# Padding the rows of one matmul operand and moving three others by a few bytes

## The chip, the cores and the metric

The kernel runs on one core of a Trainium2 chip. The metric is the device time of one execution, in microseconds (us). Three runs of the kernel before took 2669.15, 2674.47 and 2677.79 us; their median is 2674.47.

## The reference, cut to what matters

One layer of a decoder for 256 prompt tokens and 32 sample tokens (8 sequences of 4), 288 columns in all, at width 2048. Three sub-layers follow one another, each modulated (shift, scale, gate) by a conditioning vector:

```
sh1, sc1, gt1, sh2, sc2, gt2, sh3, sc3, gt3 = adaln_params(c, w_ada, b_ada)
x = x + MACARON * gt1 * swiglu(modulate(x, g_ffn1, sh1, sc1), w1_ffn1, w3_ffn1, w2_ffn1)
heads, state = mixer(modulate(x, g_mix, sh2, sc2))
x = x + gt2 * (heads @ w_out)
x = x + MACARON * gt3 * swiglu(modulate(x, g_ffn2, sh3, sc3), w1_ffn2, w3_ffn2, w2_ffn2)
```

`modulate` is an RMS norm with a gain and a shift, `swiglu(h, w1, w3, w2)` is `(silu(h @ w1) * (h @ w3)) @ w2` with an inner width of 5504 (43 tiles of 128). The mixer projects to q, k and v, attends with eight forgetting heads and eight dilated-window heads over the prompt or over a cache of 1024 tokens, and joins the heads. All is float32.

## The kernel before, in words

**Layout.** Features lie on the 128 partitions, tokens along the free dimension, so an activation is a tile of 16 k-tiles (2048 / 128) by T = 288 columns. `x` is the residual. A normalized activation is kept as two parts whose sum is its value: `h_hi` (rounded to the matmul's format, float32r) and `h_lo` (what is left), each [128, 16, 288] (L172). The inner activation of a feed-forward has the same form in `g_hi` and `g_lo`, up to 15 k-tiles of 288 columns (L190). A weight tile lands in `raw` (two slots of 16 x 128 columns), ScalarE writes its rounded part to `w_hi` (`split_high`, L867), VectorE the rest to `w_lo` (`split_low`, L1095).

**The product.** For each output tile of 128 features and for each k-tile, TensorE makes three products into one bank (`products`, L556 to L565): `w_hi` with `h_hi` (L562), `w_hi` with `h_lo` (L563), `w_lo` with `h_hi` (L564). Each loads a weight slice of 128 columns (512 bytes a partition) and then streams 288 columns (1152 bytes a partition). In the second half of a feed-forward `g_hi` and `g_lo` stand in place of `h_hi` and `h_lo`.

**Stages.** The conditioning parameters first (about 110 us), then the first feed-forward with the rest of the conditioning between its products, in three chunks of 15, 14 and 14 inner tiles, each an `up` and a `down` part (to 1089 us), the projections (1103 to 1433), the attention (to 1724), the output projection (to 1830), and the second feed-forward (1844 to 2670). `up`, projections and output projection read h, `down` reads g.

**What orders it.** Each engine runs its own program, and semaphores that the kernel names itself (L275 to L283) are the only waits between engines; nothing is derived from tiles. SP issues the weight loads in the order of their use, two slots ahead.

**Memory.** `at` (L157) puts a tile at a given byte of each partition, and `sb` (L160) takes the next free byte and rounds the tile's size up to 32 bytes. So every tile's address follows from the order and sizes of the calls: `x`, `h_hi`, `h_lo`, `par`, the constants, `raw`, `w_hi`, `w_lo`, then at `mix0` (L188) `g_hi`, `g_lo` and the rest. Before, in bytes of a partition: `h_hi` 34944, `h_lo` 53376, `w_hi` 97472, `w_lo` 113856, `g_hi` 130240, `g_lo` 147520, and the end at 229376. The attention lays its own tiles over parts that are idle then: `kv_raw` and `kv_high` over the rings from `raw` on, `kv_h` over the upper halves of `h_hi` and `h_lo`, `kv_z` over `mix0`.

**Small scalars.** `nw4`, `eps`, `bfs`, `mx`, `nm`, `sm`, `rs`, `pmx` and `psm` are one to four columns each (L180 to L266): norm weights, a constant, and the maxima and sums of the attention's softmax. Each takes 32 bytes of its own.

**Writers of h_hi.** In the norms ScalarE copies four k-tiles at once (L900) and VectorE subtracts (L1127); in the attention single k-tiles and blocks of 16 columns are written (L1016, L1069, L1324, L1411).

Of the kernel before, what the change touches and what calls it, by code (L numbers as in the profile page):

```python
# [31 lines left out]
F32R = mybir.dt.float32r  # L32
# [5 lines left out]
P = 128  # L38
D = 2048
KT = D // P  # L40
HEADS, HD = 8, 128
TP, NB, NS = 256, 8, 4
TS = NB * NS
T = TP + TS
FF = 43
CHUNKS = ((0, 15), (15, 14), (29, 14))
NPAR = 9
# [98 lines left out]
def decoder_layer(nc, xT, cT, gT, bada, nwT, bfg, relb, pt, cst, cst2, ohrev, addrev, selh,  # L146
# [7 lines left out]
    with ExitStack() as ctx:  # L154
        top = [16512]

        def at(name, shape, dt, off):  # L157
            return nc.alloc_sbuf_tensor_at(name, shape, dt, offset=off)

        def sb(name, shape, dt=F32):  # L160
            n = int(np.prod(shape[1:])) * 4
            t = at(name, shape, dt, top[0])
            top[0] += -(-n // 32) * 32
            return t
# [4 lines left out]

        x = sb("x", [P, KT, T])  # L170
        h0 = top[0]
        h_hi, h_lo = sb("h_hi", [P, KT, T], F32R), sb("h_lo", [P, KT, T], F32R)  # L172
        par = sb("par", [P, ADA * NC])
        c0 = top[0]
        sc32 = sb("sc32", [P, KT, 32])
        lf = at("lf", [HEADS, T], F32, c0)
        cs = sb("cs", [P, C_SMALL])
        gv = sb("gv", [P, 3, KT])
        ba = sb("ba", [P, ADA])
        nw4 = sb("nw4", [P, 4])  # L180
        nw = sb("nw", [P, 32])
        eps = sb("eps", [P, 1])
        ident, ones, sel9 = cs[:, C_ID:C_ID + P], cs[:, C_ONE:C_ONE + P], cs[:, C_SEL:C_SEL + NC]

        rings0 = top[0]
        raw = sb("raw", [P, 2, KT * P])
        w_hi, w_lo = sb("w_hi", [P, 2, KT * P], F32R), sb("w_lo", [P, 2, KT * P], F32R)
        mix0 = top[0]  # L188

        g_hi, g_lo = sb("g_hi", [P, 15, T], F32R), sb("g_lo", [P, 15, T], F32R)  # L190
        adaw = sb("adaw", [P, 2, KT * P])
        part_sb = sb("part_sb", [P, 4 * P])
        su, gf = sb("su", [P, T]), sb("gf", [P, T])
        hf = sb("hf", [P, 2, SQL, T])
        sq = sb("sq", [P, 2, SQL, T])
# [40 lines left out]
        def quad(name, *offs):  # L236

            n = GB // len(offs)
            parts = [at(f"{name}_{i}", [P, n, HEADS * P], F32, o) for i, o in enumerate(offs)]
            return [parts[j // n][:, j % n, :] for j in range(GB)]  # L240
        half = HEADS * T * 4
# [3 lines left out]
        first_v = at("kv_first_v", [P, 2, HEADS * P], F32, vn0)  # L245
        first = [first_v[:, 0, :], first_v[:, 1, :], at("kv_first_a", [P, HEADS * P], F32, hf0)[:, :],
                 at("kv_first_b", [P, HEADS * P], F32, sel0 + 5120)[:, :]]
        third = [quad("kv_h", h0 + half, h0 + 3 * half), quad("kv_z", mix0)]
        assert GB // 2 * HEADS * P * 4 <= half

        def kv(m, j):
# [8 lines left out]
        qbd = [sb("qbd0", [P, 2, 288]), at("qbd1", [P, 2, 288], F32, over + 13440)]  # L260
        assert 32768 + 13440 + 2304 <= 6 * KT * P * 4
        lft = at("lft", [P, 3, HEADS], F32, c0 + T * 4)
        bfs = sb("bfs", [HEADS, 1])
        rbs = sb("rbs", [32, HEADS])
        mx, nm, sm, rs = sb("mx", [P, 2]), sb("nm", [P, 2]), sb("sm", [P, 2]), sb("rs", [P, 2])
        pmx, psm = sb("pmx", [P, 2, 2]), sb("psm", [P, 2, 2])  # L266
        rev_dram = nc.dram_tensor("rev_dram", [HEADS, P, REV], F32).ap()

        pairs = [ctx.enter_context(nc.psum_tensor(f"banks{i}", [P, 2, 512], F32)) for i in range(4)]
# [1162 lines left out]
def _tiles(w, k, n):  # L1432

    return np.ascontiguousarray(w.reshape(k, P, n, P).transpose(2, 1, 0, 3).reshape(n, P, k * P))
# [62 lines left out]
def _lay_out(i):  # L1497
# [6 lines left out]
    def up(w1, w3):  # L1504
        return np.ascontiguousarray(np.stack([_tiles(w1[0], KT, FF), _tiles(w3[0], KT, FF)], 1).reshape(2 * FF, P, KT * P))

# [18 lines left out]
                                   .reshape(ADA, P, KT * P)),  # L1525
        w13_1=up(a["w1_ffn1"], a["w3_ffn1"]), w2_1=_tiles(a["w2_ffn1"][0], FF, KT),
        w_in=_tiles(cat(cols, 1), KT, 49), w_out=_tiles(a["w_out"][0], KT, KT),
        w13_2=up(a["w1_ffn2"], a["w3_ffn2"]), w2_2=_tiles(a["w2_ffn2"][0], FF, KT),

# [38 lines left out]
```

## Time and profile before

| what | value |
|---|---|
| median of three runs | 2674.47 us |
| profiled execution, first to last instruction | 2673.7 us, 0.8 us under that median |
| TensorE matmuls busy | 2522.4 us (94%) |
| weight loads busy | 2321.7 us (87%) |
| VectorE, ScalarE busy | 1159.7 us (43%), 919.7 us (34%) |
| mean granted TensorE clock | 0.962 |
| DMA moved | 614.13 MB, 230 GB/s in the mean |

The profile is of one execution and holds no other time of it than that span. Matmuls overlap in it: each lasts some 295 ns by the records, but the next one starts after some 132 ns, so what a product costs is read from the distance between starts, not from durations. Weight loads overlap the matmuls of the product before.

### The profile page before, as it was taken

What the parts mean: (1) busy time and instruction counts of PE and PEld (TensorE: products, weight loads), DVE (VectorE), ACT (ScalarE), POOL (GpSimd) and SP (SyncE); (2) the same over time, 40 slices, a digit from 0 to 9 for tenths busy, and PEclk for the clock granted to TensorE, in tenths of its full rate; (3) what the DMA queues carried; (4) which work ended last, traced back from release to release, by engine and by line L of the source; (5) the groups of instructions that cost most, each with busy time, mean ns of one, the idle gap of its engine ahead of it and who ended that gap; (6) DMA issues with size and microseconds to landing.
All of it is one profiled execution on the core that took longest, in us unless ns stands there. A gap on an engine that the chain in (4) does not pass through costs nothing.

```text
span 2673.7 us, 53818 instructions
## 1 busy us (share of the span) xinstructions
PE 2522.4 (94%) x20995; PEld 2321.7 (87%) x20995; DVE 1159.7 (43%) x1767; ACT 919.7 (34%) x1155; POOL 44.6 (2%) x86
## 2 busy tenths in 40 slices
PE   6898999999999999899999777797999999999999
PEld 3597999999999999799997343597999999999999
DVE  0343444444444445666652111255444544454444
ACT  1432323233333334566541112245333333333332
POOL 0130000000000000000000000000000000000000
PEclk7798999999999999999999878898999999999999
DMA  8887777777767764344456999943444444454444
GB/s 355 341 313 230 286 267 286 275 283 267 289 219 281 277 230 162 128 157 150 164 210 256 389 361 408 349 161 125 161 168 165 165 165 165 159 171 165 165 159 159
DMA packets 105867, 614.13 MB, mean 230 GB/s; under 512 B 16192, under 2 KB 16464, under 8 KB 56128
## 3 DMA queue, kind: packets, MB, share of 16 engines
q1 hardware_dynamic: 101728, 603.81, 61.5%
q0 software_dynamic: 4064, 9.26, 1.3%
q8 instruction: 54, 0.88, 0.1%
q14 instruction: 21, 0.17, 0.0%
HBM read 604.36 MB, written 8.66 MB: 229 GB/s over the span
## 4 chain that ended last, share of the span: by engine, by line
PE 87%; DMA 8%; SPq 2%; DVE 1%; ACT 1%; issue 1%; ACTq 0%; DVEq 0%
PE banks L562 26%; PE banks L563 25%; PE banks L564 25%; PE banks L503 4%; DMA adax<-in_w_ada_dram 2%; PE banks L830 1%; PE banks L787 1%; DMA adaw<-in_w_ada_dram 1%; SPq L440 1%; DMA kv_raw<-in_vpool_dram 1%; PE banks L514 1%; DMA raw<-in_w_dram 1%; PE banks L649 1%; PE banks L661 0%; PE banks L773 0%
## 5 line engine op out<-in xcount | busy, mean ns | idle before, releaser
L562 PE MATMUL banks<-h_hi,w_hi 128*128 128x288 f32 x3792 | 1129.1, 298 | 28.6 <-DVE h_lo L1127 23.1
L563 PE MATMUL banks<-h_lo,w_hi 128*128 128x288 f32 x3792 | 1122.6, 296 | 0.0
L564 PE MATMUL banks<-h_hi,w_lo 128*128 128x288 f32 x3792 | 1121.2, 296 | 0.0
L1095 DVE TENSOR_TENSOR w_lo<-raw,w_hi 128x1024 fp32r<-128x1024 f32 (+2 forms) x666 | 763.8, 1188 | 378.7 <-ACT w_hi L867 372.4
L867 ACT ACTIVATE w_hi<-raw 128x1024 fp32r<-128x1024 f32 (+2 forms) x666 | 667.8, 1030 | 554.0 <-PE banks L564 507.3
L562 PEld LDWEIGHTS banks<-h_hi,w_hi 128*128 128x128 f32 x3792 | 717.0, 189 | 50.2 <-issue 43.7
L563 PEld LDWEIGHTS banks<-h_lo,w_hi 128*128 128x128 f32 x3792 | 716.9, 189 | 0.8
L564 PEld LDWEIGHTS banks<-h_hi,w_lo 128*128 128x128 f32 x3792 | 716.3, 189 | 0.0
L562 PE MATMUL banks<-g_hi,w_hi 128*128 128x288 f32 x1376 | 409.2, 297 | 0.0
L563 PE MATMUL banks<-g_lo,w_hi 128*128 128x288 f32 x1376 | 406.8, 296 | 0.0
L564 PE MATMUL banks<-g_hi,w_lo 128*128 128x288 f32 x1376 | 406.6, 296 | 0.0
L562 PEld LDWEIGHTS banks<-g_hi,w_hi 128*128 128x128 f32 x1376 | 259.5, 189 | 5.4 <-issue 5.4
L563 PEld LDWEIGHTS banks<-g_lo,w_hi 128*128 128x128 f32 x1376 | 259.5, 189 | 0.0
L564 PEld LDWEIGHTS banks<-g_hi,w_lo 128*128 128x128 f32 x1376 | 259.5, 189 | 0.0
L908 ACT ACTIVATE part_sb<-banks 128x256 f32<-128x256 f32 (+1 forms) x64 | 26.3, 410 | 438.1 <-PE banks L503 438.1
L936 ACT ACTIVATE su<-banks 128x288 f32<-128x288 f32 x86 | 35.4, 412 | 403.6 <-PE banks L564 403.6
L1204 DVE TENSOR_TENSOR gf<-su,banks 128x288 f32<-128x288 f32 x86 | 39.1, 454 | 225.5 <-PE banks L564 225.5
L1149 DVE TENSOR_TENSOR par<-banks,ba 128x18 f32 (+3 forms) x64 | 11.5, 179 | 276.2 <-PE banks L514 276.2
L503 PE MATMUL banks<-adaw,sc 128*32 128x256 f32 x1792 | 112.2, 391 | 12.8 <-DMA adaw<-in_w_ada_dram 12.8
L1193 DVE TENSOR_TENSOR tmps<-banks,par 128x32 f32<-128x32 f32 x112 | 21.4, 191 | 232.8 <-PE banks L564 232.8
L503 PEld LDWEIGHTS banks<-adaw,sc 128*32 128x32 f32 x1792 | 53.1, 111 | 53.9 <-DMA adaw<-in_w_ada_dram 13.4
L503 PE MATMUL banks<-adax,sc 128*32 128x256 f32 x512 | 49.3, 534 | 29.5 <-DMA adax<-in_w_ada_dram 29.4
(186 smaller groups left out, 1134.7 us busy)
## 6 DMA issues: line engine op xcount, KB each, us to landing
raw<-in_w_dram SPq DMA_DIRECT2D x172, 1024.0 KB, 4.8
adaw<-in_w_ada_dram SPq DMA_DIRECT2D x112, 1024.0 KB, 6.4
raw<-in_w_dram SPq DMA_DIRECT2D x64, 896.0 KB, 4.6
raw<-in_w_in_dram SPq DMA_DIRECT2D x49, 1024.0 KB, 4.8
adax<-in_w_ada_dram SPq DMA_DIRECT2D x32, 1024.0 KB, 8.3
raw<-in_w_dram SPq DMA_DIRECT2D x32, 960.0 KB, 4.7
raw<-in_w_out_dram SPq DMA_DIRECT2D x16, 1024.0 KB, 4.8
kv_raw<-in_kpool_dram SPq DMA_DIRECT2D x24, 512.0 KB, 6.0
```

What stands on the lines that cost most here:

```text
L440: sp.dma_start(kv(m, j), src.rearrange("a p n -> p (a n)"))\
L503: last = pe.matmul(ada_part[32 * j:32 * j + 32, a:a + 2 * P], sc32[:, kt, :], w[:, k * 2 * P:(k + 1) * 2 * P], start=kt < 4, stop=kt >= KT ...
L514: last = pe.matmul(ada_selp[:, c * NC:(c + 1) * NC], part_sb[:, c * P:(c + 1) * P], sel9, start=True, stop=True)
L562: pe.matmul(bank[:, 0:T], hi, m_hi[:, k, :], start=k == 0, stop=False)
L563: pe.matmul(bank[:, 0:T], hi, m_lo[:, k, :], start=False, stop=False)
L564: last = pe.matmul(bank[:, 0:T], lo, m_hi[:, k, :], start=False, stop=k == nk - 1)
L649: last = pe.matmul(ss2[:, j, 0:T], ones, sq[:, j, SQL - 1, :], start=True, stop=True)
L787: r = pe.matmul(dst(j), qbd[j // 2][:, j % 2, 32 * h:32 * h + 32], moving(j, h), start=False, stop=h == HEADS - 1, tile_position=(0, 32 * ...
L867: act.activation(w_hi[:, r, a:b], raw[:, r, a:b], ACT.Copy).then_inc(S["hi_ready"], 1)
L936: act.activation(su[:, :], acc_a[:, 0:T], ACT.Silu).then_inc(S["acc_a_read"], 1)
L1095: dve.tensor_tensor(w_lo[:, r, a:b], raw[:, r, a:b], w_hi[:, r, a:b].bitcast(F32), ALU.subtract).then_inc(S["lo_ready"], 1)
L1204: dve.tensor_tensor(gf[:, :], su[:, :], acc_b[:, 0:T], ALU.mult).then_inc(S["acc_b_read"], 1)
```

## The change

Nothing that is computed changes, and no instruction is added or taken away. `h_hi` gets rows of 290 elements instead of 288 (1160 bytes from one k-tile to the next instead of 1152), and the kernel goes on using the first 288; `h_lo` keeps 288. `mix0`, where g begins, moves up by 32 bytes. The nine small tiles become slices of one tile `few` of 24 columns, which stands before the rings. The overlay `kv_h` follows the new halves.

```diff
+TPAD = T + 2
-        h_hi, h_lo = sb("h_hi", [P, KT, T], F32R), sb("h_lo", [P, KT, T], F32R)
+        h_hi = sb("h_hi", [P, KT, TPAD], F32R)[:, :, 0:T]
+        hl0 = top[0]
+        h_lo = sb("h_lo", [P, KT, T], F32R)
...
-        nw4 = sb("nw4", [P, 4])
         nw = sb("nw", [P, 32])
-        eps = sb("eps", [P, 1])
+        few = sb("few", [P, 24])
+        nw4, eps, bfs = few[:, 0:4], few[:, 4:5], few[0:HEADS, 5:6]
+        mx, nm, sm, rs = (few[:, 6 + 2 * i:8 + 2 * i] for i in range(4))
+        pmx, psm = (few[:, 14 + 4 * i:18 + 4 * i].rearrange("p (a b) -> p a b", a=2) for i in range(2))
...
-        mix0 = top[0]
+        mix0 = top[0] + 32
+        top[0] = mix0
...
-        third = [quad("kv_h", h0 + half, h0 + 3 * half), quad("kv_z", mix0)]
+        third = [quad("kv_h", h0 + HEADS * TPAD * 4, hl0 + half), quad("kv_z", mix0)]
...
-        bfs = sb("bfs", [HEADS, 1])
         rbs = sb("rbs", [32, HEADS])
-        mx, nm, sm, rs = sb("mx", [P, 2]), sb("nm", [P, 2]), sb("sm", [P, 2]), sb("rs", [P, 2])
-        pmx, psm = sb("pmx", [P, 2, 2]), sb("psm", [P, 2, 2])
```

The addresses that follow, in bytes of a partition:

| tile | before | after |
|---|---|---|
| `h_hi`, k-tile k | 34944 + 1152 k | 34944 + 1160 k |
| `h_lo`, k-tile k | 53376 + 1152 k | 53504 + 1152 k |
| `raw` | 81088 | 81248 |
| `w_hi` | 97472 | 97632 |
| `w_lo` | 113856 | 114016 |
| `g_hi`, k-tile k | 130240 + 1152 k | 130432 + 1152 k |
| `g_lo`, k-tile k | 147520 + 1152 k | 147712 + 1152 k |

## Rows read from the trace of the kernel before

**Rows 1.** The page: span, busy tenths and clock in 40 slices, the chain that ended last.
```profile
span 2673.7 us, 53818 instructions
...
PE   6898999999999999899999777797999999999999
...
PEclk7798999999999999999999878898999999999999
...
PE banks L562 26%; PE banks L563 25%; PE banks L564 25%; PE banks L503 4%; DMA adax<-in_w_ada_dram 2%; PE banks L830 1%; PE banks L787 1%; DMA adaw<-in_w_ada_dram 1%; SPq L440 1%; DMA kv_raw<-in_vpool_dram 1%; PE banks L514 1%; DMA raw<-in_w_dram 1%; PE banks L649 1%; PE banks L661 0%; PE banks L773 0%
```

**Rows 2.** Windows by stage: stretch, its length, busy time (count) by engine, clock, DMA share, GB/s.
```profile
core 0: us, PE busy (x) PEld busy (x) DVE busy (x) ACT busy (x) POOL busy (x), PEclk, DMA share, GB/s
250.00:500.00 250.00, 250.00 (x2156) 232.06 (x2149) 104.24 (x158) 75.86 (x94) 0.00 (x0) 0.99 0.75 277
...
1443.00:1724.00 281.00, 214.36 (x2764) 124.36 (x2763) 48.95 (x177) 54.09 (x155) 0.95 (x1) 0.84 0.97 378
2136.00:2312.00 176.00, 176.00 (x1333) 176.00 (x1332) 81.00 (x97) 62.86 (x70) 0.00 (x0) 1.00 0.47 163
2314.00:2402.00 88.00, 88.00 (x662) 88.00 (x661) 46.43 (x79) 30.08 (x32) 0.00 (x0) 1.00 0.49 163
```

**Rows 3.** Groups by line, TensorE: shapes, count, busy us, mean ns. L563 and L564 repeat these.
```profile
L562 PE MATMUL banks<-h_hi,w_hi 128*128 128x288 f32 x3792 | 1129.1, 298 | 28.6 <-DVE h_lo L1127 23.1 <-DVE w_lo L1095 5.3
...
L562 PE MATMUL banks<-g_hi,w_hi 128*128 128x288 f32 x1376 | 409.2, 297 | 0.0
```

**Rows 4.** Line L562 on h, then on g: count, duration ns min/median/max, first and last start.
```profile
L562 PE MATMUL banks<-h_hi,w_hi x445: 290/293/297, 2135.8 to 2311.9; 128*128 128x288 f32 x149
...
L562 PE MATMUL banks<-g_hi,w_hi x221: 292/295/302, 2313.9 to 2401.9; 128*128 128x288 f32 x111
```

**Rows 5.** Timeline of TensorE on g: start us, duration us, line. It repeats every fourth row.
```profile
2640.14 0.29 PE L563 MATMUL banks<-g_lo,w_hi 128*128 128x288 f32 x1
2640.27 0.29 PE L564 MATMUL banks<-g_hi,w_lo 128*128 128x288 f32 x1
2640.40 0.29 PE L562 MATMUL banks<-g_hi,w_hi 128*128 128x288 f32 x1
2640.53 0.30 PE L563 MATMUL banks<-g_lo,w_hi 128*128 128x288 f32 x1
2640.68 0.29 PE L564 MATMUL banks<-g_hi,w_lo 128*128 128x288 f32 x1
...
2641.21 0.29 PE L562 MATMUL banks<-g_hi,w_hi 128*128 128x288 f32 x1
```

**Rows 6.** Timeline of TensorE on h at half clock.
```profile
1103.52 0.44 PE L564 MATMUL banks<-h_hi,w_lo 128*128 128x288 f32 x1
1103.76 0.44 PE L562 MATMUL banks<-h_hi,w_hi 128*128 128x288 f32 x1
```

**Rows 7.** Groups by line: the writes of h_hi and their like; then the wait behind them.
```profile
L1127 DVE TENSOR_TENSOR h_lo<-hf,h_hi 128x1152 fp32r<-128x1152 f32 x12 | 16.3, 1355 | 8.4 <-ACT h_hi L900 8.3
...
L1117 DVE TENSOR_TENSOR hf<-x,y 128x1152 f32<-128x1152 f32 x12 | 16.2, 1354 | 0.2
...
L900 ACT ACTIVATE h_hi<-hf 128x1152 fp32r<-128x1152 f32 x12 | 14.0, 1166 | 0.4
...
L1069 ACT ACTIVATE h_hi<-banks 128x64 fp32r<-128x64 f32 x8 | 1.3, 220 | 18.9 <-PE banks L661 18.9
...
PE banks L562 <- DVE h_lo L1127: 23.1, 4, 10.7
```

**Rows 8.** DMA issues of equal size: count, KB each, median us to landing.
```profile
kv_raw<-in_kpool_dram SPq DMA_DIRECT2D x24, 512.0 KB, 6.0
...
kv_z<-in_wink_dram SPq DMA_DIRECT2D x16, 512.0 KB, 8.9
```

**Rows 9.** Groups by line: one of the small scalars.
```profile
L1398 DVE TENSOR_REDUCE sm<-sm 128x1 f32<-128x2 f32 x4 | 0.6, 155 | 4.3 <-ACT ps L1052 4.3
```

## The prediction

> **What bounds the kernel now.** I read the page first: the span, the slices, and the chain that ended last. TensorE is busy in nearly every slice at nearly full clock, and three lines, L562 to L564, hold 76% of the chain; no DMA and no other engine comes near them [rows 1]. The reader is to see that this is a kernel whose time is the number of its products times the pace at which they start, outside one stretch.
>
> Next I read the windows by stage. In 250 to 500 us and again in 2136 to 2402 us TensorE is never idle; from 1443 to 1724 us (the decode attention) it is the DMA that is full, 0.97, and TensorE has idle time [rows 2]. So what the change does to a product counts in full outside that stretch, and what it does to a transfer counts inside it.
>
> The counts come from the groups of instructions: each of the three lines made 3792 products on h and 1376 on g, 11376 and 4128 together, all of them 128 rows by 288 columns in the same number format [rows 3]. The paces come from one line's view in two stretches with nothing but products. On h the line runs 445 times, first to last 2135.8 to 2311.9 us: 176.1 / 444 = 0.3966 us for three products, 132.2 ns each. On g it runs 221 times in 2313.9 to 2401.9: 88.0 / 220 = 0.4000, 133.3 ns each [rows 4]. Same shape, same weights ring, same engine, and yet 1.1 ns apart: what differs is where the operands lie.
>
> The timeline of g shows how. Its starts are 0.13, 0.13, 0.13 us apart and then 0.14, and that repeats with every fourth product: 2640.14 to 2640.68 and 2640.68 to 2641.21 are four steps of 0.535 us together [rows 5]. The duration view agrees: on g some matmuls last 302 ns, on h none is over 297 [rows 4]. If the long step is 140 ns (0.14 in the rows), the three short ones are (4 x 133.3 - 140) / 3 = 131.1 ns. At half clock, at 1103 us, the same products start 0.24 us apart, which is 288 columns at 1.2 GHz and nothing on top; at full clock that would be 120 ns [rows 6]. So at full clock each product pays 11 to 20 ns that the columns do not explain, and that depends at least in part on addresses.
>
> **The change part by part.** It removes and adds no instruction. It moves addresses, and I work out four effects.
>
> *Products on h.* From the allocation: all weight slices lie a multiple of 512 bytes apart. Rows of h and g begin 1152 bytes (9 x 128) apart. Counted modulo 128 bytes from the weights, g now begins at 0 and h at 64. Afterwards g and h_lo begin at 32, and row k of h_hi at 32 + 8k, since its rows are 1160 bytes apart. The trace shows two relations, 0 (133.3 ns) and 64 (132.2 ns), and neither of the new ones, so the price is bounded from both sides. Below: 120 ns, the columns alone [rows 6], -12.2 x 11376 = -139 us. Above: every step the long one, 140 ns [rows 5], +7.8 x 11376 = +89 us. I take 131.3 ns, next to g's short step, because three of four steps of g and most of h sit there and a relation that shares nothing with the two bad ones should lose the long steps and no more: -0.9 x 11376 = -10.2 us.
>
> *Products on g.* By the same argument 133.3 goes to 131.3 ns: -2.0 x 4128 = -8.3 us. Bounds: 120 ns gives -13.3 x 4128 = -55 us, 140 ns gives +6.7 x 4128 = +28 us.
>
> What is late next if products get 1% faster: the weight split on VectorE and ScalarE, busy 81 and 63 of 176 us on h, and the weight DMA, 0.47 there and 0.75 at 250 us [rows 2]. All have room for 1%, so the gain stays.
>
> A rule speaks against both terms. The rows say that two streams with equal shapes run 1.1 ns apart. The Trainium skill, "TensorE: Matmul & The Clock Gate", section "Step-by-step: what each phase is for", says that TensorE has two independent read ports, so that loading the next weights takes no read bandwidth from the running matmul. By that rule an offset between weights and rows would cost nothing and both terms would be zero. The trace disagrees by those 1.1 ns, unless something else about the addresses makes them.
>
> *Writing and reading h_hi.* The 12 ACT copies that write it in the norms write four rows of 288 with a gap of 8 bytes where they wrote 1152 in one run. VectorE shows both kinds: L1117, whose second operand is four repeats of 288, takes 1354 ns, and L1127, all of one run, 1355 [rows 7]. So I put the rows at nothing, below and above. For ScalarE no such pair stands in the trace; its bounds are 0 and one more fixed cost for each of four rows, for which the shortest ACT row, 220 ns, is a ceiling: 12 x 0.66 = 8 us, of which only what TensorE waits for in the norms, 23.1 us in 4 waits, is exposed; I take 0 [rows 7]. The attention's writes of single rows (L1016) keep their shape.
>
> *Transfers and the small tile.* The rings move by 160 bytes, so the destinations of raw, kv_raw and kv_high no longer begin at a multiple of 64 bytes. Packets and bytes stay. Landing times of equal transfers lie between 6.0 and 8.9 us over different destinations with no order that follows the address [rows 8]. Bounds: 1% of the 281 us either way, +-2.8 us; taken 0. This has no cover in that stretch, since the DMA is the bound there. The one-column and two-column scalars keep their instructions and semaphores; L1398 takes 155 ns on two columns wherever they stand [rows 9]. The waits are written by hand on semaphores, so sharing a tile adds none. Nothing.
>
> Sum: -10.2 - 8.3 = -18.5 us on the profiled execution's span of 2673.7, which lies 0.8 us under the median of the three runs, 2674.47. On the median that is 2656 us.
>
> **The rivals.**
>
> 1. *Nothing that can be measured.* The mean pace is kept by a cycle of stalls, and new offsets only order it differently: 132.2 and 133.3 stay within 0.5 ns, at most 0.5 x 15504 = 8 us. For it: g with its long steps and h without them differ by only 0.8%, so the pace hardly depends on offsets. Against it: the long step is plainly there to be removed. Time 2666 to 2682, say 2674.
>
> 2. *A large gain.* The 11 to 20 ns above the columns are all a clash of two reads, and at 32 bytes it is gone. For it: half clock shows no such excess [rows 6]. Against it: no step in the rows here is near 120. A third of the bound is -65 us, 2610; all of it, -194, 2480.
>
> 3. *Slower: the rows of h_hi no longer share a phase.* Now every row begins at the same place modulo 128, and the pattern of steps can settle. With 1160 bytes each k begins elsewhere, half of the rows at 8 modulo 16. If that gives h the cycle of g, one long step in four, h goes to 133.3: +1.1 x 11376 = +12.5 us, 2687. If every odd row of h_hi (half of 7584 products) takes the long step, it is 7.8 x 3792 = +30 us, 2704. It decides from a mean pace on h of 132.9 ns on. For it: g shows that a long step needs only another offset [rows 5]. Against it: 64 and 0 have no feature that 32 + 8k is bound to worsen.
>
> A page points the same way. The Trainium skill, "Advanced Engine Details and Errata", section "SBUF Cachelines", gives lines of 16 bytes and a penalty for changing to another line. A row of 1152 bytes then covers 72 lines from an even start and 73 from one 8 bytes in; as an estimate from that page, 1/72 of a step on 3792 products, +7 us. No run here shows such a start yet.
>
> **How the numbers follow.** Forecast, 8 to 40 us gained: 0.40. Large gain, over 40 us: 0.14. Nothing: 0.26. Slower: 0.20. A change of 0.3% (8 us) is about what a measurement of this kernel can tell from none. So faster 0.54, same 0.26, slower 0.20. The likeliest case alone reaches from 2634 to 2666. For eight in ten I leave out half of the large gains and the upper half of the slower ones: 2605 to 2690.
>
> **What would show it.** In the trace after: line L562 on g over the stretch of its products should give 0.394 us for three, with no matmul over 297 ns, and on h 0.394 as well. If g's every fourth step is still 0.14, that term is wrong; if h is above 0.3987, rival 3 holds; if either is under 0.389, rival 2. L900 above 1.2 us or a kv landing median moved by over 5% would show the terms that I put at nothing. The prediction is wrong if the paces move and the time does not, which would mean that a wait took the gain.

## The result: slower by half a percent, and the profile after

The changed kernel takes 2689.29 us in the median of four runs (2687.06 to 2689.87), the kernel before 2675.56 us (2669.15 to 2677.79). The ratio is 1.0055, 95% interval 1.0041 to 1.0070: some 14 us slower, where 18.5 us faster was forecast. The time lies at the upper end of the range and beside the 2687 us of the third rival.

The page of the changed kernel (lines are three further down, so that L562 to L564 are L565 to L567 now):

```profile
span 2687.2 us, 53818 instructions
...
PE 2528.8 (94%) x20995; PEld 2332.2 (87%) x20995; DVE 1159.7 (43%) x1767; ACT 919.4 (34%) x1155; POOL 44.5 (2%) x86
...
L565 PE MATMUL banks<-h_hi,w_hi 128*128 128x288 f32 x3792 | 1142.5, 301 | 29.3 <-DVE h_lo L1130 22.8
```

Little else on the page has moved: counts are equal, and VectorE and ScalarE are as busy as before. The place to look is the pace. The view of line L565 over the stretch of h, then of g, that answers to [rows 4] (count, duration ns min/median/max, first and last start):

```profile
L565 PE MATMUL banks<-h_hi,w_hi x445: 291/297/302, 2146.0 to 2324.0; 128*128 128x288 f32 x149
...
L565 PE MATMUL banks<-g_hi,w_hi x222: 292/295/298, 2325.6 to 2414.0; 128*128 128x288 f32 x111
```

On h 178.0 us over 444 steps of three products is 133.6 ns a product, where it was 132.2; the longest matmul lasts 302 ns, where it was 297. On g 88.4 over 221 is 133.3 ns, as before, although its longest matmul went from 302 to 298 ns. Were this so in every stretch, the 11376 products on h would pay 1.4 ns more, 15.9 us, and the 4128 on g nothing. The span grew by 13.5 us. The start times of the two traces close the gap: in the first feed-forward, where the conditioning's products stand between, h went only from 132.3 to 133.3 ns. Summed stretch by stretch at full clock, the products on h took 13.8 us more and those on g 0.6.

The timeline of g (start us, duration us) answers to [rows 5]:

```profile
2339.72 0.30 PE L566 MATMUL banks<-g_lo,w_hi 128*128 128x288 f32 x1
2339.86 0.29 PE L567 MATMUL banks<-g_hi,w_lo 128*128 128x288 f32 x1
2339.99 0.30 PE L565 MATMUL banks<-g_hi,w_hi 128*128 128x288 f32 x1
2340.12 0.29 PE L566 MATMUL banks<-g_lo,w_hi 128*128 128x288 f32 x1
2340.26 0.30 PE L567 MATMUL banks<-g_hi,w_lo 128*128 128x288 f32 x1
```

Before, one matmul in four lasted 0.30; now every second one does, and four steps still take 0.54 us. By the start times, a cycle on g was three steps of 130 to 132 ns and one of 140; now steps of 131 to 132 and of 135 take turns. The long step is gone, and the time that it cost has been spread over the others.

On h, in the stretch of [rows 4], the start times before show no long step at all: all but three of 1341 steps are 131 to 134 ns. After, they lie between 126 and 141 ns.

The terms that were put at nothing, in the windows by stage (columns as in [rows 2]), the groups and the DMA issues ([rows 7, 8]):

```profile
1447.00:1731.00 284.00, 208.80 (x2768) 121.80 (x2766) 48.94 (x177) 53.72 (x155) 0.95 (x1) 0.87 0.97 379
2146.00:2324.00 178.00, 178.00 (x1335) 178.00 (x1333) 80.89 (x96) 62.74 (x70) 0.00 (x0) 1.00 0.46 162
```

```profile
L903 ACT ACTIVATE h_hi<-hf 128x1152 fp32r<-128x1152 f32 x12 | 14.0, 1168 | 0.4
```

```profile
kv_raw<-in_kpool_dram SPq DMA_DIRECT2D x24, 512.0 KB, 6.4
...
kv_z<-in_wink_dram SPq DMA_DIRECT2D x16, 512.0 KB, 9.6
```

The granted clock of the products on h is 1.00, as before, so the pace is not the clock's doing. ScalarE writes four padded rows in 1168 ns where it took 1166. In the attention the DMA moves 379 GB/s where it moved 378, with the queue full either way. These two landings are up by 0.4 and 0.7 us, 7 and 8%, and the one that rose most, kv_raw from in_wink_dram, went from 8.3 to 10.3; that is over the 5% that the prediction named as the sign of a cost. The cost did not come: from the last product of the projections to the first of the output projection it is 292.6 us, where it was 293.9.

### The profile page after: what moved, and what is told of

The parts are those of the page before. It is cut to its first block, busy times and chain, and to the rows that moved or that the text cites. A ratio compares the mean times of both kernels' runs of the same rounds, so it can differ in the third digit from the quotient of the medians.

```text
span 2687.2 us, 53818 instructions
## 1 busy us (share of the span) xinstructions
PE 2528.8 (94%) x20995; PEld 2332.2 (87%) x20995; DVE 1159.7 (43%) x1767; ACT 919.4 (34%) x1155; POOL 44.5 (2%) x86
## 4 chain that ended last, share of the span: by engine, by line
PE 87%; DMA 8%; SPq 2%; DVE 1%; ACT 1%; issue 1%; ACTq 0%; DVEq 0%
PE banks L565 26%; PE banks L567 25%; PE banks L566 25%; PE banks L506 4%; DMA adax<-in_w_ada_dram 3%; DMA kv_h<-in_vpool_dram 1%; PE banks L833 1%; SPq L443 1%; PE banks L790 1%; DMA adaw<-in_w_ada_dram 1%; DMA kv_raw<-in_wink_dram 1%; DMA kv_z<-in_wink_dram 1%; PE banks L517 1%; PE banks L652 1%; SPq L434 1%
## 5 line engine op out<-in xcount | busy, mean ns | idle before, releaser
L565 PE MATMUL banks<-h_hi,w_hi 128*128 128x288 f32 x3792 | 1142.5, 301 | 29.3 <-DVE h_lo L1130 22.8
L566 PE MATMUL banks<-h_lo,w_hi 128*128 128x288 f32 x3792 | 1124.1, 296 | 0.0
L567 PE MATMUL banks<-h_hi,w_lo 128*128 128x288 f32 x3792 | 1122.6, 296 | 0.0
L565 PEld LDWEIGHTS banks<-h_hi,w_hi 128*128 128x128 f32 x3792 | 716.3, 189 | 50.9 <-issue 44.9
L566 PEld LDWEIGHTS banks<-h_lo,w_hi 128*128 128x128 f32 x3792 | 721.1, 190 | 0.8
L567 PEld LDWEIGHTS banks<-h_hi,w_lo 128*128 128x128 f32 x3792 | 719.5, 190 | 0.0
L565 PE MATMUL banks<-g_hi,w_hi 128*128 128x288 f32 x1376 | 410.0, 298 | 0.0
L566 PE MATMUL banks<-g_lo,w_hi 128*128 128x288 f32 x1376 | 407.6, 296 | 0.0
L567 PE MATMUL banks<-g_hi,w_lo 128*128 128x288 f32 x1376 | 407.5, 296 | 0.0
L565 PEld LDWEIGHTS banks<-g_hi,w_hi 128*128 128x128 f32 x1376 | 259.3, 188 | 5.4 <-issue 5.4
L566 PEld LDWEIGHTS banks<-g_lo,w_hi 128*128 128x128 f32 x1376 | 259.4, 188 | 0.0
L567 PEld LDWEIGHTS banks<-g_hi,w_lo 128*128 128x128 f32 x1376 | 259.3, 188 | 0.0
```

The lines of the kernel that those rows point to most:

```text
L565: pe.matmul(bank[:, 0:T], hi, m_hi[:, k, :], start=k == 0, stop=False)
L566: pe.matmul(bank[:, 0:T], hi, m_lo[:, k, :], start=False, stop=False)
L567: last = pe.matmul(bank[:, 0:T], lo, m_hi[:, k, :], start=False, stop=k == nk - 1)
```

## The experiments

The terms used below: the distance of a row is the byte at which it begins, minus that of the weight slice, modulo 128. Before it was 64 for h and 0 for g; the change makes it 32 for g and h_lo and 32 + 8k for row k of h_hi. Paces of whole kernels come from line views like the one above, over the second feed-forward. The letters A to D and F are theories that the expectations state. Edits are against the changed kernel in the first three runs and in the padding alone, and against the kernel before in the others.

### Four parts alone

**The shift of h_lo without the pitch.**

```diff
-        h_hi = sb("h_hi", [P, KT, TPAD], F32R)[:, :, 0:T]
+        h_hi = sb("h_hi", [P, KT, T], F32R)
+        top[0] += 128
```

> The changed kernel with one part undone: rows of h_hi are 1152 bytes apart again, but h_lo keeps its new place 128 bytes later, and rings and g stay where the change put them. In the trace of the changed kernel three products on h take 0.4008 us (133.6 ns each) where they took 0.3966 (132.2), and g is as before (133.3). Theory A, halves: a product is slow where h_hi and h_lo of the same k-tile begin in different halves of 256 bytes, as g_hi and g_lo always did. Then the 128 bytes alone do it: h at 133.3 ns, some 12 us over the kernel before. Theory B, pitch: rows of 1160 bytes do it; then h is back at 132.2 and the time within 3 us of before. Theory C, weights: the distance of rows from weights modulo 64 does it; then h stays at 133.6, some 14 us over.

```profile
L566 PE MATMUL banks<-h_hi,w_hi x446: 293/296/298, 2150.9 to 2328.8; 128*128 128x288 f32 x149
```

177.9 / 445 / 3 = 133.3 ns. Time 1.0057 of before (1.0039 to 1.0074): as slow as the changed kernel. The pitch is not needed for the loss, so B as it was put falls. A and C both still stand.

**The pitch with both operands in the same half.**

```diff
-        h_hi = sb("h_hi", [P, KT, TPAD], F32R)[:, :, 0:T]
-        hl0 = top[0]
-        h_lo = sb("h_lo", [P, KT, T], F32R)
+        hl0 = top[0]
+        h_lo = sb("h_lo", [P, KT, T], F32R)
+        h0 = top[0]
+        h_hi = sb("h_hi", [P, KT, TPAD], F32R)[:, :, 0:T]
```

> The changed kernel with h_lo and h_hi allocated in the other order: h_lo at 34944 and h_hi at 53376 with rows of 1160 bytes, so that both begin in the same half of 256 bytes for every k; rings and g stay where the change put them. A, halves: h at 132.2 ns, time within 4 us of the kernel before. B, pitch: h at 133.6, some 14 us over. C, weights: 133.6, some 14 us over.

```profile
L566 PE MATMUL banks<-h_hi,w_hi x445: 292/296/300, 2152.8 to 2329.9; 128*128 128x288 f32 x149
```

177.1 / 444 / 3 = 133.0 ns, time 1.0055 (1.0038 to 1.0072). A alone asked for 132.2 and does not fit; 133.0 is none of the three numbers. The pace accounts for only 0.8 x 11376 = 9 of the 15 us: in this run's trace the stretch from the last product of the projections to the first of the output projection takes 301 us, against 294 before. Over all traces of the layer it takes 292 to 301 and does not follow where the rings lie: the changed kernel, with the same rings, has 293.

**The rings and g alone.**

```diff
-        h_hi = sb("h_hi", [P, KT, TPAD], F32R)[:, :, 0:T]
+        h_hi = sb("h_hi", [P, KT, T], F32R)
         hl0 = top[0]
         h_lo = sb("h_lo", [P, KT, T], F32R)
+        top[0] += 128
...
```

The overlay `kv_h` follows here.

> Only the rings and g are moved as in the change; h_hi and h_lo have the addresses and the rows of the kernel before. A and B: h at 132.2 ns and g at 133.3, time within 3 us of before. C, weights: h at 133.6, some 14 us over.

Line L566 over the second and the third chunk's products on h:

```profile
L566 PE MATMUL banks<-h_hi,w_hi x447: 294/294/297, 2150.0 to 2329.9; 128*128 128x288 f32 x149
...
L566 PE MATMUL banks<-h_hi,w_hi x447: 294/296/297, 2420.3 to 2598.7; 128*128 128x288 f32 x149
```

179.9 / 446 / 3 = 134.5 ns and 178.4 / 446 / 3 = 133.3 ns; time 1.0068 (1.0051 to 1.0084). With h_hi and h_lo exactly where they were before, moving the weights by 160 bytes is enough: C holds, A and B fall. And the two stretches run the same instructions on the same addresses at different paces, so addresses allow more than one pace. What picks one is not shown.

**g_lo moved by 128 bytes in the kernel before.**

```diff
-        g_hi, g_lo = sb("g_hi", [P, 15, T], F32R), sb("g_lo", [P, 15, T], F32R)
+        g_hi = sb("g_hi", [P, 15, T], F32R)
+        top[0] += 128
+        g_lo = sb("g_lo", [P, 15, T], F32R)
...
```

To make room, seven of the small scalars share one tile here, behind everything that a product reads; the runs `f1_weights48` and `f3_g64` below do the same.

> The kernel before with g_lo 128 bytes later (nothing else that a product reads is moved; the small scalars after the end of the activations share one tile to make room), so that g_hi and g_lo of a k-tile begin in the same half of 256 bytes. A, halves: g goes from 133.3 to 132.2 ns, 4128 times 1.1 ns, some 4.5 us under the kernel before. B, pitch, and C, weights: g stays at 133.3, no change.

```profile
L565 PE MATMUL banks<-g_hi,w_hi x223: 288/296/298, 2317.0 to 2405.8; 128*128 128x288 f32 x112
```

88.8 / 222 / 3 = 133.3 ns, time 1.0012 (0.9998 to 1.0026): no change. A falls once more. The distance of g is 0 modulo 128 here as before, as C needs. The shared tile of scalars costs nothing that can be measured either.

### Two maps of the pace

To see the rule itself, TensorE was run alone on other addresses. Each loop is this, with three turns; W, H and L stand for its addresses, "..." for the flags of the accumulation, and loops on the addresses of g have 14 k-tiles:

```
for j in range(2):
    for k in range(16):
        w, hi, lo, b = W + 8192 * j + 512 * k, H + 1152 * k, L + 1152 * k, banks[j][:, 0:288]
        pe.matmul(b, at(w, P), at(hi, 288), ...)
        pe.matmul(b, at(w, P), at(lo, 288), ...)
        pe.matmul(b, at(w + 16384, P), at(hi, 288), ...)
```

> Nothing of the layer is computed here: TensorE alone runs the three products of the kernel (same shapes, two weight slots, two banks) in 57 loops of 2 tiles x 16 k-tiles x 3 passes, each loop with other addresses of the weights, of the first and of the second operand; the other engines are idle. Its total time means nothing, the mean distance between starts within each loop does. If operand addresses alone set the pace, the loops with the addresses of the kernels repeat their paces: h before 132.2 ns, g before 133.3, h after 133.6, rings moved alone 133.3 to 134.4; if other engines' accesses matter, they don't. Theory C, distance of rows from weights: moving the weights by d bytes and moving both rows by -d give the same pace, and 64 modulo 128 is the fast one. Theory D, where the weight slice itself begins modulo 64: moving the weights by 32 makes it slow, moving the rows does nothing. Theory F, a cycle that locks on its history: equal addresses at the first and the last loop may differ, and the pace follows no address. Columns: if the 12 ns over the columns' own time are a fixed cost of a product, 256 columns take 118.9 ns and 512 take 225.5; if the weight load bounds the pace, 256 columns still take 130 or more and 512 take 215.

> As the first map, nothing of the layer is computed: 62 loops of products with other operand addresses, TensorE alone. Rule under test, from the first map: with rows that begin at a multiple of 32 bytes and lie 1152 apart, the pace follows the distance of the rows from the weight slices modulo 128 bytes: 64 gives 132.2 ns, 0 and 32 and 96 modulo 64 give 132.2 or 133.3, 16 and 80 give 131.1. By the rule: rows of g moved by 64 give 132.2 with the weights where they are, 133.3 with the weights at +32, and 131.1 with the weights at +48 or +112; rows +32 with weights +80, and rows +64 with weights +112, are distance 16 and give 131.1; rows +16 with weights +64 are distance 16 too, but begin at a 16: 131.1 if distance is all, above 132 if the beginning of the row counts as well. Rows of 1160 bytes for h_hi with the weights back at distance 64: 132.2 if the pitch costs nothing by itself, 132.9 (as in the first map) if it costs 0.7. A rival, that the paces are an accident of one loop, falls if the first loop, its repeat at the end and the repeats of +48 and +112 come out as before.

Lines of the first map, one a loop, where 95 steps of three products lie between first and last start. In this order: addresses of the kernel before with the weights at +32, +48, +64, +80; the rings moved alone; both rows moved by 192; 256 columns; 512 columns; and the addresses before, repeated last.

```profile
L209 PE MATMUL banks<-rows x96: 293/295/298, 413.4 to 451.4; 128*128 128x288 f32 x96
...
L218 PE MATMUL banks<-rows x96: 292/293/297, 451.8 to 489.2; 128*128 128x288 f32 x96
...
L227 PE MATMUL banks<-rows x96: 293/295/297, 489.6 to 527.6; 128*128 128x288 f32 x96
...
L236 PE MATMUL banks<-rows x96: 295/297/302, 528.0 to 566.3; 128*128 128x288 f32 x96
...
L164 PE MATMUL banks<-rows x96: 294/296/298, 222.2 to 260.2; 128*128 128x288 f32 x96
...
L353 PE MATMUL banks<-rows x96: 288/296/297, 1024.9 to 1062.9; 128*128 128x288 f32 x96
...
L551 PE MATMUL banks<-rows x96: 278/279/284, 1838.3 to 1871.6; 128*128 128x256 f32 x96
...
L614 PE MATMUL banks<-rows x96: 387/390/393, 2116.0 to 2181.5; 128*128 128x512 f32 x96
...
L623 PE MATMUL banks<-rows x96: 292/294/295, 2182.2 to 2219.9; 128*128 128x288 f32 x96
```

Such a line gives the pace to some 0.3 ns (38.0 / 285 = 133.3, 37.4 / 285 = 131.2, 38.3 / 285 = 134.4, 37.7 / 285 = 132.3). The start times of the same traces give it finer; over the last two thirds of each loop the mean distance between starts is, in ns:

| distance of the rows | 64 | 48 | 40 | 32 | 16 | 0 | 112 | 96 | 80 |
|---|---|---|---|---|---|---|---|---|---|
| weights moved by | 0 | 16 | 24 | 32 | 48 | 64 | 80 | 96 | 112 |
| ns a product | 132.22 | 132.78 | 132.22 | 133.33 | 131.11 | 133.33 | 134.44 | 132.22 | 131.11 |

| loop with the addresses of | map | in the kernel |
|---|---|---|
| h before, first map's last loop | 132.22 | 132.2 |
| g before | 133.33 | 133.3 |
| h after | 133.61 | 133.6 |
| g after | 133.33 | 133.3 |
| rings moved alone | 133.33 | 133.3 and 134.5 |
| h with the shift of h_lo, no pitch | 133.33 | 133.3 |

A lone TensorE repeats these paces, all but the 134.5 of one stretch, so they need no other engine's access and no transfer. With rows laid out as those of h, moving the weights one way or both rows the other way is the same: weights +64 and rows +192 give 133.33 both, weights +96 and rows +160 give 132.22 both, and +128 of either is back at 132.22. So in these loops it is the distance that counts, modulo 128; D, the weights' own address, falls. F falls in its plain form, since the repeated loops agree (132.22 in both maps, +48 and +112 at 131.11 in both).

The column loops fit neither of the two ideas put ahead: 116.7 ns for 256 columns and 230.0 for 512, where a fixed cost wanted 118.9 and 225.5 and a bound by the weight load 130 or more and 215. The excess over the columns' own time at full clock, 106.7 and 213.3, is 10.0 and 16.7. Addresses count here as well: with the weights at +48 the second map has 118.9 and 230.7.

Lines of the second map: rows of 1160 for h_hi with the distance of before; rows +32 with weights +80 (distance 16); rows +16 with weights +64 (distance 16 too); rows of g +64 with weights +48, then with weights +112; `h_lo` alone +128 with weights +48. The last line is of the first map: rows 1280 bytes apart.

```profile
L506 PE MATMUL banks<-rows x96: 289/296/302, 1621.0 to 1658.9; 128*128 128x288 f32 x96
...
L461 PE MATMUL banks<-rows x96: 292/293/298, 1430.4 to 1467.8; 128*128 128x288 f32 x96
...
L470 PE MATMUL banks<-rows x96: 289/295/296, 1468.2 to 1505.8; 128*128 128x288 f32 x96
...
L389 PE MATMUL banks<-rows x84: 292/293/294, 1162.8 to 1195.1; 128*128 128x288 f32 x84
...
L434 PE MATMUL banks<-rows x84: 293/296/300, 1329.6 to 1362.9; 128*128 128x288 f32 x84
...
L560 PE MATMUL banks<-rows x96: 293/294/298, 1850.5 to 1888.2; 128*128 128x288 f32 x96
...
L515 PE MATMUL banks<-rows x96: 290/293/298, 1684.8 to 1722.8; 128*128 128x288 f32 x96
```

From the start times: 133.06, 131.11, 131.67, 130.00, 133.33, 132.50 and 133.33 ns. So the pitch of 1160 costs 0.84 at the distance of before. Rows that begin at a 16 have other paces than their distance gives: 131.67 for 131.11 at 16, and in the first map 132.22 for 134.44 at 112.

The rule of distance does not carry over to g, though its rows begin at multiples of 32 too. At 0, 32 and 64 they agree with those of h, but at 16 they have 130.00 for 131.11, at 80 (weights +112) 133.33 for 131.11, and at 96 133.3 for 132.22; the expectation of 131.1 at 16 and 80 was missed both times. Nor is it the distance alone on h: with the weights at +48, `h_lo` 128 bytes later gives 132.50 for 131.11, and rows 1280 bytes apart, ten times 128, leave every distance at 64 and give 133.33 for 132.22. So where the two rows lie to one another and from one k-tile to the next counts as well, and the runs give no rule for that.

Pitches of 1168, 1184 and 1216 for both rows gave 132.08, 132.22 and 132.22 at the distance of before. With the weights at +48, where 1152 has 131.11, they gave 132.4, 132.2 and 131.11. So 1168 and 1184 are free at one distance and cost over 1 ns at another.

### The rule in whole kernels

**The padding alone, all distances as before.** Here `few` stands at the end, the rings 64 bytes later than they would then begin, and `mix0` without its 32 bytes.

```diff
-        few = sb("few", [P, 24])
+        few = at("few", [P, 22], F32, 229280)
...
+        top[0] += 64
         rings0 = top[0]
...
-        mix0 = top[0] + 32
+        mix0 = top[0]
```

> The padding of h_hi alone: rows of 1160 bytes, h_lo 128 bytes later, and the weights and g moved so that every distance modulo 128 bytes is that of the kernel before (64 for h_lo and the first row of h_hi, 0 for g); the small scalars stand behind the other tiles. If the 32 bytes of distance explained all, h is at 132.2 and the time within 3 us of before. If the pitch costs something by itself, as the second map has it (133.06 at these addresses): 11376 x 0.84 = some 9.5 us over, g unchanged at 133.3.

```profile
L567 PE MATMUL banks<-h_hi,w_hi x446: 289/296/302, 2146.0 to 2323.7; 128*128 128x288 f32 x149
```

177.7 / 445 / 3 = 133.1 ns, time 1.0046 (1.0032 to 1.0059). By these paces the pitch costs 0.9 x 11376 = 10 us of these 12.

**g at the distance of h.**

```diff
-        mix0 = top[0]
+        mix0 = top[0] + 64
+        top[0] = mix0
```

> The kernel before with g alone 64 bytes later, so that its rows stand at distance 64 from the weights, as those of h do. By the maps g goes from 133.3 to 132.2 ns, 4128 x 1.1 = 4.6 us under the kernel before, h unchanged; by the theory that g is slow for its two halves (which the run with g_lo moved already speaks against) nothing changes.

```profile
L564 PE MATMUL banks<-g_hi,w_hi x221: 290/293/295, 2308.6 to 2395.9; 128*128 128x288 f32 x111
```

87.3 / 220 / 3 = 132.3 ns, time 0.9971 (0.9958 to 0.9984): 8 us faster, 4 to 11, where 4.6 was expected.

**Weights 48 bytes later, g 64 bytes later.**

```diff
-        w_hi, w_lo = sb("w_hi", [P, 2, KT * P], F32R), sb("w_lo", [P, 2, KT * P], F32R)
+        wts = sb("wts", [P, 4 * KT * P + 16], F32R)
+        w_hi, w_lo = (wts[:, 12 + n * 2 * KT * P:12 + (n + 1) * 2 * KT * P].rearrange("p (r n) -> p r n", r=2) for n in range(2))
...
-        over = rings0 + 32768
+        over = rings0 + 32768 + 64
```

> The kernel before with the weight slices 48 bytes later and g 64 bytes later, rows of h as they were (1152 apart). The second map has 131.1 ns for h and 130.0 for g at these addresses. If what the maps show of a lone TensorE holds beside working engines and transfers: h 131.1, g 130.0, so 11376 x -1.1 and 4128 x -3.3 = -12.5 - 13.8 = some 26 us under the kernel before. Rival, that the kernel's other stages or the weight split take it back: under 8 us. Rival, that the maps do not carry over: paces stay between 132 and 134, no change.

```profile
L564 PE MATMUL banks<-h_hi,wts x445: 292/293/298, 2124.1 to 2298.8; 128*128 128x288 f32 x149
...
L564 PE MATMUL banks<-g_hi,wts x222: 292/294/298, 2299.9 to 2387.8; 128*128 128x288 f32 x111
```

h at 174.7 / 444 / 3 = 131.2 ns, as mapped; g at 87.9 / 221 / 3 = 132.6, not the 130.0 of the map. The time is 2662.41 us against 2676.1, ratio 0.9959 (0.9944 to 0.9974): some 11 us, 7 to 15, under the kernel before. Some 26 us had been expected. By the paces, 11376 x 1.0 + 4128 x 0.7 = 14 us; most of what is missing is g, (132.6 - 130.0) x 4128 = 11 us. It is the fastest of the versions by its median; whether it beats the one with g alone moved, 2667.85, these intervals do not tell.

## Why the prediction was wrong

*The bound was read rightly.* The pace of the products accounts for the time: 13.8 us on h and 0.6 on g, against a span that grew by 13.5.

*The step that failed is the value taken for both terms.* The prediction took 131.3 ns because "a relation that shares nothing with the two bad ones should lose the long steps and no more". That treats the long step as a stall on top of a fixed short step. On g the long step did go, and the mean stayed at 133.3 ns to the tenth: every second step grew to 135. The short step of a slow cycle is not the pace of another cycle. For h the ground was misread as well: "most of h" does not sit at 131.3. Of those 1341 steps on h before, 298 are 131 ns and nearly all others 132 to 134, so h had no long step to lose. The bounds, 120 and 140 ns, held; the choice between them was a guess. It had the wrong sign for h (+13.8 us measured, -10.2 forecast), and for g it forecast -8.3 us where +0.6 was measured.

*The relation was a right quantity, but not the only one.* The distance modulo 128, which the prediction worked out from the addresses, does set the pace where the layout is that of h. But 32 is one of the slow distances, 133.33, as slow as 0; 16 and 80 are the fast ones on h. On g 80 is slow, and with other pitches the distance is not enough. Nothing in the trace before could tell that, since it held only 64 and 0.

*The third rival was right in its place; its price was in part luck.* It asked for a pace on h over 132.9 because rows of 1160 bytes keep no common phase, and gave 2687 us. The padding alone does that (133.1 ns, 1.0046), though not by the cycle of g, one long step in four, from which the price came: the steps scatter from 125 to 141 ns. And it is half the story: the move of the weights alone slows h too (133.3 to 134.5), and the two together give 133.6, not their sum.

*The first rival's reason was not right.* On g the mean was kept only because 32 happens to be as slow as 0: at 64 g runs at 132.3 (`f3_g64`). On h it was not kept.

*The two pages.* Weights moved alone in steps of 16 bytes, rows fixed, gave anything from 131.11 to 134.44 ns. The Trainium skill, "TensorE: Matmul & The Clock Gate", section "Step-by-step: what each phase is for", has two read ports that do not take bandwidth from each other; by that rule these loops would be equal, and the trace disagrees by up to 3.3 ns in 132. At the distance of before, rows of 1160 bytes, half of which begin 8 bytes into 16, cost 0.84 ns, and rows of 1168, which do not, nothing. The Trainium skill, "Advanced Engine Details and Errata", section "SBUF Cachelines", has lines of 16 bytes and a penalty for an access to a different one; the estimate from it was a loss of some 7 us, and the run with the padding alone agrees in sign, with about 10. That the lines are the reason is not shown: with the weights at +48, rows of 1168 cost 1.3 ns too.

*What stays open.* Why an address costs anything is not shown: that the read of the weights and the read of the rows wait for each other is only argued, since every product here loads its weights. Why g runs at 132.6 in the kernel and at 130.0 in the map on the same addresses, and why one kernel ran equal code on equal addresses at 133.3 and 134.5, is not settled. In the kernel a semaphore wait stands in the middle of each tile, in the map none does; that it picks the cycle is only argued.

## What to carry to other kernels

Where a stream of equal products runs slower than its columns, look at the distance between the two operands' addresses too, and measure it on the very layout that the kernel has: a loop of a few hundred products on chosen addresses mostly gave the pace of a 2.7 ms kernel to a tenth of a nanosecond. Then measure the kernel: on g the loop had 130.0 where the kernel had 132.6. Do not take the shortest step of a repeating pattern as the price without the stall; only the mean over the pattern is a price. And a pad or a merged tile moves everything behind it, so the cost of what was moved by accident belongs in the sum.

## What was not expected of the hardware

With all addresses fixed, the pace settles on a value that a repeating pattern of steps makes; in many of the loops it is one of 131.11, 132.22, 133.33 and 134.44 ns, which lie 1.11 apart. With rows as those of h, moving the weights alone is worth up to 4.4 ns of 132 a product (131.11 at +48, 135.55 at +84 bytes), 3% of the time of products, from operands that are otherwise equal. Moving one operand by 128 bytes is free at some addresses and costs 1.4 ns at others. The excess over the columns' own time is larger at 512 columns, 16.7 ns, than at 256, 10.0.
